# Prompt's attention: the values of the next pair of heads spread over all four units of a pair, each unit but the first beginning with one

## The reference

```python
v = jnp.einsum('btr,rhv->bthv', c_kv, w_uv)       # values of all heads from the latents (256 wide)
s = jnp.einsum('bqhd,bkhd->bhqk', qi, k) * SCALE
s = jnp.where(k_pos[None, :] <= q_pos[:, None], s, -jnp.inf)
p = jax.nn.softmax(s, axis=-1)
o = jnp.einsum('bhqk,bkhv->bqhv', p, v)
```

## Time and profile before

| | |
|---|---|
| median of 3 runs | 2108.0 us (2107.07 to 2108.83) |
| profiled execution | 2109.14 us, span 2107.3 us |
| granted PE clock, mean | 0.995 |
| PE busy | 2063.0 us (98%) |
| DVE, ACT, POOL busy | 1173.9, 814.4, 384.7 us |
| units 0 to 11 of the prompt's attention | from 425.47 us, to about 578 us |

### The profile page before, as it was taken

One profiled execution on the slowest core, in us unless ns is written; L12 is line 12 of the kernel. 1 busy time (PEld: TensorE's weight loads), 2 busy tenths in 40 slices (PEclk: granted clock), 3 DMA queues, 4 the chain that ended last, 5 costly groups with the idle time before them and its releaser, 6 DMA issues.

```text
span 2107.3 us, 35218 instructions
## 1 busy us (share of the span) xinstructions
PE 2063.0 (98%) x12669; PEld 1902.2 (90%) x12669; DVE 1173.9 (56%) x2357; ACT 814.4 (39%) x1589; POOL 384.7 (18%) x441
## 2 busy tenths in 40 slices
PE   7999999999989999999999999999999999999999
PEld 6889999988879999999999978899998999999997
DVE  5673411277766777767776754544444444444444
ACT  5552111265644656656665742312112212112111
POOL 2210000144520245534553520000000000000000
PEclk9999999999998999999999999999999999999999
DMA  4332222335313122222222170111111111111102
GB/s 169 88 106 70 62 85 93 112 105 156 91 61 89 43 68 64 66 66 69 68 61 73 52 249 21 61 50 51 40 40 40 40 47 53 40 48 52 40 20 85
DMA packets 146272, 152.43 MB, mean 72 GB/s; under 512 B 50711, under 2 KB 122119, under 8 KB 145102
## 3 DMA queue, kind: packets, MB, share of 16 engines
q1 hardware_dynamic: 140405, 128.02, 20.5%
q0 software_dynamic: 5728, 22.65, 3.3%
HBM read 124.77 MB, written 25.97 MB: 72 GB/s over the span
## 4 chain that ended last, share of the span: by engine, by line
PE 66%; DVE 2%; ACT 1%; issue 1%; DVEq 0%
PE ps L104 19%; PE ps L106 19%; PE ps L105 19%; PE ps L1498 2%; PE ps L1457 1%; PE ps L1463 1%; PE ps L2115 1%; DVE ss L1649 0%; DVE cTl L1655 0%; ACT sq L1567 0%; PE ps L2069 0%; DVE var L1725 0%; PE ps L2113 0%; PE ps L2116 0%; PE ps L1555 0%
## 5 line engine op out<-in xcount | busy, mean ns | idle before, releaser
L104 PE MATMUL ps<-mh,f_w1h 128*128 128x384 f32 (+1 forms) x768 | 250.6, 326 | 0.0
L106 PE MATMUL ps<-mh,f_w1l 128*128 128x384 f32 (+1 forms) x768 | 250.5, 326 | 0.0
L105 PE MATMUL ps<-ml,f_w1h 128*128 128x384 f32 (+1 forms) x768 | 250.3, 326 | 0.0
L2143 ACT ACTIVATE tail_room<-ps 128x384 f32<-128x384 f32 (+1 forms) x96 | 45.5, 474 | 502.1 <-PE ps L106 502.1
L2188 DVE TENSOR_TENSOR t_m<-t_m,ps 128x512 f32<-128x512 f32 x256 | 172.8, 685 | 114.4 <-PE ps L106 114.4
L1567 ACT ACTIVATE sq<-ps 128x512 f32<-128x512 f32 x256 | 153.2, 598 | 208.1 <-PE ps L106 208.0
L105 PE MATMUL ps<-f_late_l,f_late_h 128*128 128x512 f32 x512 | 199.8, 390 | 0.0
L106 PE MATMUL ps<-f_late_h,f_late_l 128*128 128x512 f32 x512 | 199.7, 390 | 0.0
L104 PE MATMUL ps<-f_late_h 128*128 128x512 f32 x512 | 199.4, 389 | 0.0
L2168 DVE TENSOR_TENSOR tail_room<-tail_room 128x384 f32<-128x384 f32 (+1 forms) x96 | 51.5, 536 | 253.7 <-ACT tail_room L2143 253.7
L104 PE MATMUL ps<-wq,cTh 128*128 128x320 f32 x512 | 172.0, 336 | 2.5 <-DVE g_attn_b L1647 2.1
(11 more groups left out here) (353 smaller groups left out, 5010.5 us busy)
## 6 DMA issues: line engine op xcount, KB each, us to landing
f_raw<-in_w_ff SPq DMA_DIRECT2D x32, 1024.0 KB, 5.2
c_ring<-in_cache_kv_latent SPq DMA_DIRECT2D x192, 128.0 KB, 2.0
m_raw<-in_w_in SPq DMA_DIRECT2D x20, 512.0 KB, 3.8
gated<-gate POOLq DMA_DIRECT2D x8, 1088.0 KB, 4.9
pa_gm<-gated SPq DMA_DIRECT2D x16, 512.0 KB, 4.6
c_early<-in_cache_kv_latent SPq DMA_DIRECT2D x64, 128.0 KB, 2.0
fr_x<-in_x_prompt SPq DMA_DIRECT2D x8, 512.0 KB, 3.5
mixed<-pa_mixed SPq DMA_DIRECT2D x16, 256.0 KB, 2.0
```

Of the source, the lines that this page charges most:

```text
L104: nc.tensor.matmul(out, lh, rh, start=first, stop=False)
L105: nc.tensor.matmul(out, lh, rl, start=False, stop=False)
L106: return nc.tensor.matmul(out, ll, rh, start=False, stop=last)
L2143: nc.scalar.activation(z[:, a, 0:w], ps[:, 2 * par + a, 0:w], ACT.Relu).then_inc(S["relu"], 1)
```

## The change

`phase_items` gives the nine values of the next pair to all four units of a pair, 3, 2, 2 and 2, instead of five to the first and four to the third. In the first unit of a pair each value still follows a block; in the other three each value precedes one. `apart` is 2 for lists of 7 items or more, where it was 9.

```diff
-        if qc == 0 and h // 2 + 1 < H // 2:
-            values = [("value", h // 2 + 1, i) for i in (range(5) if h % 2 == 0 else range(5, NK))]
+        if h // 2 + 1 < H // 2:
+            share = (range(0, 3), range(3, 5), range(5, 7), range(7, NK))[u % 4]
+            values = [("value", h // 2 + 1, i) for i in share]
         out = []
         while blocks or values:
-            out += blocks[:1] + values[:1]
+
+            out += (blocks[:1] + values[:1]) if u % 4 == 0 else (values[:1] + blocks[:1])
             blocks, values = blocks[1:], values[1:]
         return out
...
-        apart = 2 if len(todo) >= 9 else 1
+        apart = 2 if len(todo) >= 2 * NT - 1 else 1
```

## The result

The changed kernel took 2119.59 us (median of 5 runs, 2117.8 to 2120.14) against 2108.65: a ratio of 1.0051, 95% interval 1.0036 to 1.0066. It is slower, as forecast (2116.0), by 10.9 us where 8.0 were worked out. The profiled execution has a span of 2117.8 us, 10.5 more than the one before.

The account below looks back on a forecast made before the run. PE was taken as busy almost all of the span, so only its waits count. Three groups of 1.05 + 1.6 us made 8.0 us, 2117.1 from the profiled 2109.14; the median, 1.1 lower, was forecast at 2116.0, range 2107.5 to 2122.

Parts of the forecast that it names:

- PE's work is constant, the waits decide: Whole kernel: every instruction stays, only order changes, so time changes by PE's waits alone; idle some 15 us, not 7.
- Unit 0 can't be shorter than its chain: Units 0 to 1: softmax chain ending on POOL unchanged, so b0 of unit 1 waits 1.25 us, coming 0.1 us sooner.
- The list of what would show it: Expected profile signs, units 0 to 11: six transpose waits for POOL, about 1.0 to 1.3 us each; waits before b7, b3.
- the first step of the sum: Entry of odd units: b0 waits for POOL's scaling; in units 0 to 1 this leaves unit 1 1.0 us more to do.
- Moved work: Units 0 to 1: v4 (0.79 us) and the product of b3 (0.29) are still to do when b0 starts.
- The gate: Odd units: a value's low part queues behind DVE's gate, so PE waits 0.95 us at b7; bounds 0 and 1.2.
- The gate under POOL's subtraction: Unit 2: the gate's second operation starts some 0.3 us later but keeps its end, 0.54 us behind POOL's subtraction.
- Units 2 to 3: Second pair of each group: +0.15 for b0, +0.79 for v8, +0.95 for the gate, -0.3 for old idle: +1.6 us.
- the term set at nothing: Units 12 to 15: without values, they keep their order and two longest waits, 1.90 and 2.83 us; no change counted.
- A: Units 0 to 11: ACT and DVE, freed of values, finish the softmax sooner; -0.6 us, 2107.4; chance 0.08.
- B: Units 0 to 11: values move the waits, but the gate's is hidden; +2.3 us, 2110.3; chance 0.22.
- C: Units 1, 2 and 3 of each group: new waits lower PE's clock; 2131, or 2121 if one in three; chance 0.10.

## Why the prediction was right, step by step

*PE's work is constant, the waits decide.* Right in the main: 975 and 976 matmul rows in units 0 to 11, and idle 14.7 us, "some 15" in the prediction. But 2.0 of the 8.87 us are in PE's busy time, where the prediction had none.

*Unit 0 can't be shorter than its chain.* Right in time: b0 of unit 1 stands 13.85 us behind the start of unit 0, 13.87 before. The wait's place was wrong. The prediction had all of it at b0; it overlooked that the first score of a head waits for POOL's k, so 0.82 us stand ahead of the score and the rest is covered. The list of what would show it said six waits of transposes for POOL; there are two of those, 0.5 us each, and six waits of a score, 0.3 to 1.0 us. By the prediction's own sign ("If b0 of odd units doesn't wait for POOL, the first step of the sum is wrong") this step failed at b0 of units 1, 3, 7 and 11. That the sum for units 0 to 1 held all the same is in part luck: on POOL the last scaling starts as k's subtraction ends (437.23 and 437.24), so PE is held until about the same time by either.

*Moved work.* v4 and the product of b3, 1.08 us by the prediction; units 0 to 1 came out at +1.16, +1.12, +1.16 where 1.05 was the sum. Right.

*The gate.* 0.95 us in front of b7; measured 0.83 to 0.85, six times, within its bounds. 0.7 in front of b3, which the sum left out; measured 0.45 to 0.51.

*The gate under POOL's subtraction.* In unit 2 its second operation starts later and still ends with POOL, now 1.04 us long; DVE's and POOL's timelines of the change:

```profile
458.10 1.04 DVE L1187 TENSOR_TENSOR pa_mixed<-pa_mixed,pa_gm 128x512 f32<-128x512 f32 x1
```

```profile
456.15 2.44 POOL L1063 TENSOR_TENSOR pa_ql<-pa_raw_q,pa_qh 96x1024 fp32r<-96x1024 f32 x1
```

459.14 against 458.59, 0.55 behind it (0.54 before): right.

*Units 2 to 3.* +1.6 by the sum, +1.81 measured. b0 of unit 3 came 0.29 later, counted from the start of unit 2 (465.35 - 450.09, against 464.01 - 449.04), not 0.15, and not by the scaling that the prediction had. POOL's and PE's timelines of the change:

```profile
460.63 2.45 POOL L1063 TENSOR_TENSOR pa_kl<-pa_raw_k,pa_kh 96x1040 fp32r<-96x1040 f32 x1
463.06 1.78 POOL L1079 TENSOR_SCALAR pa_prob<-pa_prob,pa_rden 128x784 f32<-128x784 f32 x2
```

```profile
465.35 0.60 PE L1286 MATMUL ps<-ident,pa_prob 128*128 128x128 f32 x4
```

The last scaling ends at 464.84, which is 0.08 sooner from the start of unit 2 than before (463.87): the slack on POOL took the whole delay. b0 comes 0.51 us behind it, where it came 0.14 behind it before. What held it was k: the head's first score could start only at 463.18, and that score, v7 and a product, 2.17 us of PE's own work, stood between it and b0.

*The sum.* 8.0 for units 0 to 11, 8.87 measured: work moved behind POOL and the gate's waits were right, k's wait was missing, and both pairs' terms came out a little small. The rest of the 10.9 us is the term set at nothing: the clock behind the old, long waits of units 12 to 15, 1.6 us of difference between two profiles and 2 us between two profiles of the same kernel. What share of the medians' difference it has is not settled; the runs of the change spread over 2115.4 to 2120.1, and units 0 to 11 are alike to 0.02 us in its two profiles.

*The rivals.* A (the chain gets faster) did not happen: from the start of unit 2, POOL's k ended 0.36 us later than before (463.08, against 461.67) and the last scaling only 0.08 sooner. B (the gate hidden) did not either. C did not in units 0 to 11 of the changed kernel, but in two of its neighbours.

## What to carry to other kernels

Even where PE is busy nearly all of the span, filler work is not free to be spread evenly: ask of each stretch which chain sets its length, and take filler out only where PE does. Here the even units were as long as a chain over DVE, ACT and POOL, and what moved the time the right way was a link of that chain, put where its engine had nothing else to do. An item put first in a list also lands behind whatever another engine does at that place.

## What the runs showed of the hardware that was not expected

Where the clock fell did not go by the length of a wait. It fell behind pairs of 1.27 and 1.01 us (462.1 to 465.4 with the share kept and the block first) and of 1.02 and 1.58 (486.7 to 491.4 with shares 2, 3, 2, 2). It stayed at 1.00 behind a single wait of 2.02 at 437.03 in that same run, behind 1.02, 0.29 and 0.49 in the change, and behind 1.71 and 1.50 some 7 us apart with the gate later. Behind one wait of 1.9 us it fell in one profile of the change and not in the next. Behind the longest wait, at the entry of unit 15, it stayed at 1.00 in the profile before (2.83 us) and fell in both of the change (2.87 us; 0.57 and 0.62 over the 4 us from the wait's end), so what rival C reads from that row is one execution's. The single wait of 2.02 and the window behind it, then the window behind the 2.87 in the first profile of the change:

```profile
437.03 0.36 PE L104 MATMUL ps<-pa_kh,pa_qh 96*128 96x264 f32 x1 [2.02 <-POOL pa_kl L1063]
437.00:441.00 4.00, 3.97 (x31) 3.96 (x32) 2.00 (x5) 2.05 (x6) 2.62 (x5) 1.00 0.75 205
```

```profile
620.60:624.60 4.00, 3.96 (x20) 3.78 (x21) 0.86 (x2) 1.21 (x3) 0.00 (x0) 0.57 0.12 41
```

By the mean clock of such a stretch of two units, the falls are an estimated 1.6 us (27.35 x 0.06) to 3.4 (31.02 at a mean of 0.89); the second is too high, as part of it lies in PE's idle time. PE's busy time in these two stretches grew by 1.4 and 2.5 us against the change.

A wait of PE for POOL's `k_lo` was recorded as "issue" in some places (0.28 to 1.00 us) and under POOL's name in others (0.96 to 2.02): an "issue" row can be a semaphore.
